# Up projection with tokens and their rests side by side in one product per weight tile

## The reference

```python
D_MODEL = 1024
SEQ = 256
D_FF = 2816
CONV_WIDTH = 3
...
        h = rms_norm(x, g_pre_ffn[i])
        u = causal_depthwise_conv(h @ w_up[i], conv_w[i], conv_b[i])
        gate, val = jnp.split(u, 2, axis=-1)
        f = (jax.nn.gelu(gate, approximate=True) * val) @ w_down[i]
        x = x + rms_norm(f, g_post_ffn[i])
```

## Time and profile before

| | |
|---|---|
| median of 3 runs | 942.58 us (941.62 to 947.96) |
| profiled execution | 944.15 us, of which the span is 942.4 us |
| TensorE busy | 789.0 us (84%) |
| VectorE, ScalarE, GpSimd busy | 348.7, 313.3, 125.5 us |
| up projection | from 147.2 to 275.4 us |
| down projection | from 275.4 to about 335 us |

### The profile page before, as it was taken

The page is one execution under the profiler, slowest core; times in us unless marked ns, Lnnn a source line. Parts: engine busy times, 40 slices in busy tenths (PEclk is TensorE's granted clock), DMA queues, the critical chain, the costliest instruction groups (busy, mean ns, idle before and its releaser), DMA issues.

```text
span 942.4 us, 12391 instructions
## 1 busy us (share of the span) xinstructions
PE 789.0 (84%) x5204; PEld 523.6 (56%) x5204; DVE 348.7 (37%) x767; ACT 313.3 (33%) x623; POOL 125.5 (13%) x129
## 2 busy tenths in 40 slices
PE   9999999999999999999899997557665576756765
PEld 7985578999998867778786443113220222211213
DVE  6746765777765554398523011010100101001002
ACT  5665655766665476313632100001000000000012
POOL 0011031444441042101311000000000000000000
PEclk9999999999999999999999998989888988788868
DMA  9955971755534476544559999999999999999995
GB/s 352 408 213 216 431 301 54 276 188 190 187 124 179 179 268 248 222 179 160 198 206 411 403 428 426 428 428 428 427 428 428 428 427 428 427 429 426 430 426 208
DMA packets 24110, 297.95 MB, mean 316 GB/s; under 512 B 2672, under 2 KB 3056, under 8 KB 5488
## 3 DMA queue, kind: packets, MB, share of 16 engines
q1 hardware_dynamic: 24048, 297.09, 77.3%
HBM read 296.03 MB, written 1.05 MB: 315 GB/s over the span
## 4 chain that ended last, share of the span: by engine, by line
PE 58%; DMA 32%; DVE 4%; ACT 4%; issue 1%; POOL 0%; DVEq 0%; ACTq 0%; POOLq 0%
PE ps L107 58%; DMA ring<-in_exps 32%; ACT fr L116 1%; DVE ar L125 1%; ACT ar L116 1%; PE ps L110 1%; ACT ar L113 1%; DVE misc L148 1%; ACT sq L113 1%; DVE fr L125 0%; DVE yT L125 0%; DVE yT L129 0%; DVE sq L130 0%; DVE rb L136 0%; DVE hT L133 0%
## 5 line engine op out<-in xcount | busy, mean ns | idle before, releaser
L107 PE MATMUL ps<-ring,sq 128*32 128x512 f32 x944 | 137.7, 719 | 74.1 <-DMA ring<-in_exps 73.7
L107 PE MATMUL ps<-fr 128*128 128x256 f32 (+1 forms) x956 | 164.8, 325 | 1.1 <-DVE fr L125 1.1
L107 PEld LDWEIGHTS ps<-fr 128*128 128x128 f32 x956 | 141.6, 192 | 16.9 <-ACT fr L116 1.2
L107 PE MATMUL ps<-ring,ar 128*32 128x512 f32 (+3 forms) x792 | 104.0, 614 | 45.1 <-DMA ring<-in_exps 39.3
L107 PEld LDWEIGHTS ps<-ring,sq 128*32 128x32 f32 x944 | 28.7, 121 | 171.1 <-DMA ring<-in_exps 117.7
L125 DVE TENSOR_TENSOR ar<-ar,ps 128x512 f32<-128x512 f32 x9 | 6.2, 688 | 255.1 <-PE ps L107 255.1
L125 DVE TENSOR_TENSOR fr<-ring,fr 128x512 fp32r<-128x512 f32 (+1 forms) x96 | 77.7, 828 | 50.6 <-ACT fr L116 50.3
L116 ACT ACTIVATE ar<-ps 128x512 f32<-128x512 f32 (+4 forms) x48 | 27.2, 571 | 176.1 <-PE ps L110 142.5
L107 PEld LDWEIGHTS ps<-ring,ar 128*32 128x32 f32 (+1 forms) x792 | 27.2, 119 | 104.5 <-DMA ring<-in_exps 58.4
L116 ACT ACTIVATE fr<-ring 128x512 fp32r<-128x512 f32 (+1 forms) x114 | 66.6, 624 | 26.3 <-PE ps L107 23.6
L107 PE MATMUL ps<-ar 128*128 128x512 f32 (+9 forms) x320 | 64.1, 420 | 10.9 <-DVE ar L125 10.1
(11 more groups left out here) (188 smaller groups left out, 928.2 us busy)
## 6 DMA issues: line engine op xcount, KB each, us to landing
ring<-in_exps SPq DMA_DIRECT2D x86, 2048.0 KB, 30.9
ring<-in_modw SPq DMA_DIRECT2D x12, 2048.0 KB, 8.9
ring<-in_wup SPq DMA_DIRECT2D x11, 2048.0 KB, 9.1
ring<-in_wdown SPq DMA_DIRECT2D x5, 2048.0 KB, 7.6
ar<-in_exps SPq DMA_DIRECT2D x5, 2048.0 KB, 12.8
ring<-in_win SPq DMA_DIRECT2D x4, 2048.0 KB, 7.6
ring<-in_exps SPq DMA_DIRECT2D x6, 1024.0 KB, 8.1
ring<-in_wo SPq DMA_DIRECT2D x2, 2048.0 KB, 9.9
```

Of the source, the lines that this page charges most:

```text
L107: return Issue(self.e and self.e.matmul(o, l, r, start=start, stop=stop, skip_group_check=True))
```

## The change

Each weight tile is loaded twice a step in place of three times. `wh` is multiplied with XH and XL at once (one product of 512 moving columns: 256 tokens' rounded parts, then their rests, from two places 2048 columns apart), then `wl` with XH alone (256 columns). So a tile m fills a whole bank: the left half holds `wh*xh + wl*xh`, the right half `wh*xl`. A round takes four banks, and two rounds take all eight. The halves are added afterwards: ScalarE copies the right halves of a part to `sq` (`up_half`, 128 x 512), and VectorE adds the left halves from PSUM (`up_total`, 128 x 512, signal "u"). The base and the taps now read that sum in `sq`. TensorE waits for "u" of round j - 2 in place of its taps. The steps of the convolution move: the halves and totals are step 2, bases 3 and 4, taps 3 to 6, gelu 6, "f" 7, and `f_hi` with `f_lo` become a step 9, which stands in step 1 of the round after. The down projection takes banks 2 to 5 and the embedding of `p` banks 6 and 7.

```diff
-        FB = (0, 1, 4, 5)
-        DB = {(0, 0): 2, (0, 1): 3, (1, 0): 6, (1, 1): 7}
+        UB = ((6, 0), (2, 4))
+        DB = {(0, 0): 2, (0, 1): 3, (1, 0): 4, (1, 1): 5}
+        x_parts = fr[:, XH:XH + 4096].rearrange("p (h k t) -> p h k t", h=2, t=S)
...
-                        o, c = half(up_bank(j, m // 2), m % 2), slice(128 * m, 128 * m + 128)
-                        xh, xl = tile(fr, k, XH), tile(fr, k, XL)
-                        pe.matmul(o, wh[:, c], xh, k == 0 and m % 2 == 0, False)
-                        pe.matmul(o, wh[:, c], xl, False, False)
-                        t = pe.matmul(o, wl[:, c], xh, False, k == 7)
+                        b, c = up_bank(j, m), slice(128 * m, 128 * m + 128)
+                        pe.matmul(bank(b), wh[:, c], x_parts[:, :, k, :], k == 0, False)
+                        t = pe.matmul(half(b, 0), wl[:, c], tile(fr, k, XH), False, k == 7)
...
+            def up_half(j, p):
+                b = UB[j % 2][p]
+                act.wait_ge(pe_up[j, 7], dve_up["conv", j - 1, p] if j else None)
+                act.copy(by(up_sum(p), S), ps[:, b:b + 2, S:2 * S]).then_inc(act_up, "half", j, p)
...
-                act.wait_ge(pe_up[j, 7], pool_up["f_lo", j - 2] if j > 1 else dve_up["x_lo", 7])
+                act.wait_ge(dve_up["u", j, p], pool_up["f_lo", j - 2] if j > 1 else dve_up["x_lo", 7])
...
             def conv_step(j, step):
-                if step == 1:
+                if step == 2:
+                    up_half(j, 0)
+                    up_half(j, 1)
+                elif step == 3:
                     conv_base(j, 0)
-                elif step == 3:
+                elif step == 4:
                     conv_base(j, 1)
-                elif step == 5:
+                elif step == 6:
...
-                elif step == 7:
+                elif step == 9:
...
+            def up_total(j, p):
+                b = UB[j % 2][p]
+                dve.wait_ge(pe_up[j, 7], act_up["half", j, p])
+                dve.tensor_tensor(by(up_sum(p), S), ps[:, b:b + 2, 0:S], by(up_sum(p), S), ALU.add).then_inc(dve_up, "u", j, p)
...
-                    y, u = conv_place(j, p)[:, S * i:S * i + S], half(up_bank(j, p), i)
+                    y, u = conv_place(j, p)[:, S * i:S * i + S], tile(up_sum(p), i)
```

More of the change, by code:

```diff
@@ L315, in conv_place, with up_bank, up_sum @@
             return yT[:, o:o + 512]
-        def up_bank(j, part_):
-            return FB[(2 * j + part_) % 4]
+        def up_bank(j, m):
+            return UB[j % 2][m // 2] + m % 2
+        def up_sum(part_):
+            return sq[:, 512 * part_:512 * part_ + 512]
         DOWN_ORDER = [(f, n) for f in range(20) for n in range(2)] + [(f, n) for n in range(2) for f in (20, 21)]
@@ L737, in tensor @@
                         if k == 0 and m % 2 == 0:
-                            pe.wait_ge(dve_up["conv", j - 2, m // 2] if j > 1 else
-                                       (dve_mod["mod", 1] if m // 2 else dve_mod["sum", 1]) if j else dve_joint["mix", "x", 7])
-                        o, c = half(up_bank(j, m // 2), m % 2), slice(128 * m, 128 * m + 128)
-                        xh, xl = tile(fr, k, XH), tile(fr, k, XL)
-                        pe.matmul(o, wh[:, c], xh, k == 0 and m % 2 == 0, False)
-                        pe.matmul(o, wh[:, c], xl, False, False)
-                        t = pe.matmul(o, wl[:, c], xh, False, k == 7)
+                            if j > 1:
+                                pe.wait_ge(dve_up["u", j - 2, m // 2])
+                            elif j:
+                                pe.wait_ge(*((dve_mod["sum", 1], dve_mod["mod", 1]) if m else (act_joint["mix", "rroot"], dve_up["h", 7])))
+                            else:
+                                pe.wait_ge(dve_joint["mix", "x", 7])
+                        b, c = up_bank(j, m), slice(128 * m, 128 * m + 128)
+                        pe.matmul(bank(b), wh[:, c], x_parts[:, :, k, :], k == 0, False)
+                        t = pe.matmul(half(b, 0), wl[:, c], tile(fr, k, XH), False, k == 7)
                     t.then_inc(pe_up, j, k)
@@ L753, in down @@
                 if f == 0:
-                    pe.wait_ge(act_joint["mix", "rroot"], dve_up["h", 7], dve_joint["mix", "x", 3])
+                    pe.wait_ge(dve_up["u", 9, 1])
                 pe.matmul(o, fh, wh, f == 0, False)
@@ L1367, in scalar @@
                         conv_step(j - 1, k)
+                    if j > 1 and k == 1:
+                        conv_step(j - 2, 9)
             for i, (f, n) in enumerate(DOWN_ORDER):
@@ L1374, in scalar @@
                     conv_step(10, i // 2)
+                if i == 3:
+                    conv_step(9, 9)
                 if (f, n) == (8, 1):
@@ L1387, in embedded @@
                 act.wait_ge(pe_gate["e", j, n])
-                act.copy(ar[:, o:o + 512], bank(5 + j)).then_inc(act_gate, "e", j, n)
+                act.copy(ar[:, o:o + 512], bank(6 + j)).then_inc(act_gate, "e", j, n)
             def gate_rounded(n, k):
@@ L1826, in conv_tap @@
                         dve_up, *(("tap", j, p, i) if d == 1 else ("conv", j, p)))
+            def up_total(j, p):
+                b = UB[j % 2][p]
+                dve.wait_ge(pe_up[j, 7], act_up["half", j, p])
+                dve.tensor_tensor(by(up_sum(p), S), ps[:, b:b + 2, 0:S], by(up_sum(p), S), ALU.add).then_inc(dve_up, "u", j, p)
             def conv_step(j, step):
                 if step == 2:
+                    up_total(j, 0)
+                    up_total(j, 1)
+                elif step == 3:
                     conv_tap(j, 0, 1)
-                elif step == 3:
+                elif step == 4:
                     conv_tap(j, 0, 2)
-                elif step == 4:
+                elif step == 5:
                     conv_tap(j, 1, 1)
-                elif step == 5:
+                elif step == 6:
                     conv_tap(j, 1, 2)
@@ L2145, in conv_step @@
                 g, v = conv_place(j, 0), conv_place(j, 1)
-                if step == 6:
+                if step == 7:
                     pool.wait_ge(t, act_up["gelu", j], dve_up["conv", j, 1])
                     t = pool.tensor_tensor(g, g, v, ALU.mult).then_inc(pool_up, "f", j)
-                elif step == 7:
+                elif step == 9:
                     hi, lo = (fr[:, o + 512 * j:o + 512 * j + 512] for o in (FH, FL))
@@ L2160, in gpsimd @@
                         t = conv_step(j - 1, k, t)
-            for step in (6, 7):
+                    if j > 1 and k == 1:
+                        t = conv_step(j - 2, 9, t)
+            t = conv_step(9, 9, t)
+            for step in (7, 9):
                 t = conv_step(10, step, t)
```

11 lines of the change are left out of this document (5 added, 6 removed).

## The result

The changed kernel took 950.58 us (948.4 to 953.4, 5 runs), the kernel before 942.89 us beside it. A few executions took from 1287 to 2641 us, most of them of the kernel before, and are left out of every ratio. The forecast was 946.5 us, 3.9 slower, with a range of 937.5 to 952.

What follows compares the result with a forecast made beforehand. TensorE bounds the up projection now; afterwards a 12.16 us chain leads. 8.6 us lost minus 4.7 gained is 3.9 us slower, taking the median from 942.58 to 946.5 us, range 937.5 to 952.

Steps and rivals of the forecast that it cites:

- TensorE sets the end, and a shift passes on: Up projection: only TensorE sets its end, and later loads move with compute, so a shift counts one to one.
- TensorE's saving, 4.7 us: Up projection: a step takes 1.387 us instead of 1.440, saving 0.0533 us in each of 88 steps.
- The chain from "f" to "f", 12.16 us: Up projection round: `f_hi`, `f_lo`, rest, add, bases, taps, rests and "f" take 12.16 us against TensorE's 11.09.
- Taps stopped since both inputs are in SBUF: Convolution in the up projection: eight taps a round now read two SBUF tensors, so GpSimd can stop them.
- The port's total, 11.9 us a round: Port of VectorE and GpSimd: 11.9 us asked a round, so TensorE's 11.09 is out of reach in any order.
- Eight rounds at 1.07 us: Up projection: the first three rounds keep TensorE's pace, the other eight lose 1.07 us each, 8.6 us in all.
- TensorE's pace as the faster rival: Up projection: without the last taps' 1.10 us stop the chain is 11.06 us, time 937.9 or 941.3; chance 0.24.
- A second stop: Rest of k = 3 on GpSimd also stops the taps: round 13.4 us, 13.5 us slower, 956; chance 0.10.
- No saving from the wide product: Width switches eat the saving: TensorE stays at 11.52 us a round, time 947.7; chance 0.63 together with the forecast.

Runs made afterwards that it cites:

- unsorted mixed order: Changed kernel's product order, each 512-column product followed by its 256-column one; sorting the four wide ones first, on the kernel with sum in PSUM and later `f_hi`: 939.83 us, 0.9965.
- second profile after: The changed kernel itself timed and profiled once more, with nothing altered: 951.45 us, 1.0084 of the kernel before.
- the later `f_hi`: Changed kernel with `f_hi` and `f_lo` one step later, behind the rounding of k = 2 and ahead of the two copies: 941.34 us, ratio 0.9974.
- both cures: Changed kernel with the sum of the halves kept in PSUM and `f_hi` and `f_lo` one step later: 941.29 us, ratio 0.9978.

## Why the prediction was right, and where its sizes were off

**TensorE sets the end, and a shift passes on.** Right. 5.93 us in the rounds stand against 6.6 us of time (4.5 to 8.7), and each experiment's rounds agree with its ratio within its interval.

**TensorE's saving, 4.7 us.** The mechanism was right (fewer products, no fewer columns), the size holds only for part of the time. The term "4 x (0.2267 + 0.120)" took each width's cost from a stretch where it stood alone. It came out in round 1 of the first profile after, 11.09 us, and was not kept: undisturbed rounds of the unsorted mixed order took 11.31 us everywhere else, 0.3533 us a pair. Where nothing is late, about 2.1 us are saved over ten rounds. At half clock in round 0 next to nothing is saved: with a granted clock of 0.75 from 147.2 to 154 us the first two steps took 4.43 us before and 4.42 in the second profile after. In the changed kernel this term hardly weighs, since from round 3 on the chain sets the rounds.

**The chain from "f" to "f", 12.16 us.** Right in its links, their order and its length (12.25 us measured). Each link that the prediction named stands in the trace of after, the stop of the last taps (1.06 us) and that of the rest of k = 2 by `f_lo` among them. That the chain leads is shown by the later `f_hi`, which takes the rounding and the rest of k = 2 out of it and gives 11.30 us a round, with the taps stopped as before.

**Taps stopped since both inputs are in SBUF.** Right. Shown from both sides: the kernel before with one input moved to SBUF lost 11.6 us, the kernel after with it moved back to PSUM gained 6.6.

**The port's total, 11.9 us a round, "in any order".** Wrong. With the later `f_hi` the same operations fit into rounds of 11.30 us. The sum took 1.29 us for each of GpSimd's operations, but a stop added 1.10 (2.40 us for two rests in place of 1.30); with that my estimate is 6 x 0.61 + 8 x 0.39 + 4 x 1.10 = 11.2 us.

**Eight rounds at 1.07 us.** Rounds 3 to 10 cost 98.15 us where eight of before are 92.1, 6.0 us more; the prediction had 8 x 0.64 = 5.1. Round 2 was already late by 0.7 us against 11.09: the layout left out that the first gelu loads its table, 1.28 us on ScalarE at 167.55, and the chain that ended last goes through it; what round 2 would be without it was not tried. The 0.9 and 0.7 us, and the 0.4 of round 0 that the 3.9 contain and the ten rounds do not, make up the difference between 3.9 and 5.9 us.

**TensorE's pace as the faster rival.** It did not come, for the reason that spoke against it: a stop taken from one place (the rest of k = 7) came back at another ("f"). But the 1.10 us were not the only way out: `f_hi` behind the rounding of k = 2 was enough with the stop in place. The prediction also slipped in this rival's second number: by its own sum a chain of 11.4 us gives 8 x 0.31 - 4.7 = 2.2 us faster, 940.4 us, and not "minus 1.3 or so", 941.3.

**A second stop.** From round 2 on it did not come: the rest of k = 3 on GpSimd ran beside the adds (225.35 to 226.65 us against a first tap at 226.94), with 0.29 us to spare where 0.22 were laid out. In round 1 it did, by 0.23 us (two first taps in 1.11 us and not 0.88), without making TensorE late.

**No saving from the wide product.** Undisturbed rounds took 11.31 us and not 11.52, so half of the saving was there, and at times all of it. It was, as forecast, without weight for the time, since the chain set the rounds.

## What to carry to other kernels

Before an operand moves from PSUM to SBUF, look who else is at work: a VectorE instruction with two inputs in SBUF waits for GpSimd and makes it wait (0.47 against 1.09 us in one row pair of the profile before), and one with an input in PSUM does not. Where no engine's busy time is near the bound, lay the lists of the engines out behind each other and look for the chain that closes on itself; its length is the round, and what helped here was to take a link or a stop out of it (one step's delay of `f_hi`, or the sum in PSUM), and moving work from GpSimd to VectorE did not. Take the cost of a product from a row with the same neighbours: the saving of 0.0133 us a product, read from two uniform stretches, was twice what most mixed rounds gave.

## What the runs showed of the hardware

GpSimd can wait for more than one VectorE instruction. Its operation of 1.29 us took 1.6 us beside a first rest and got in ahead of the second (changed kernel, 220.92 us), but 2.78 us beside a run of three rests and 2.18 beside a run of two, behind all of them. The Trainium skill, "SBUF — State Buffer", section "SBUF: two separate sides", has the pair of ports held "for the whole instruction"; by that GpSimd would get in behind the first rest and take some 1.6 us, 1.2 less than was seen. In the changed kernel GpSimd began 0.22 us behind VectorE's first rest and had stood idle for 0.82 us, in the others 0.25 or 0.26 us behind and idle for 3.3 to 5.5 us. Whether one of these decides was not tried.

TensorE's start at half clock differs between executions: from 147.2 to 154 us the granted clock was 0.75 before, 0.50 in the first profile after, 0.75 in the second, and 1.00 with both cures, and round 0 took from 11.4 to 13.9 us with it. The same instructions stood ahead of it.
